# The down projection of an encoder layer in another order of its seven block products

## The reference, cut to what matters

```python
def encoder_forward(x, ...):
    h = rmsnorm(x, norm_mix); z = h @ w_in
    a = pool_mixer(z[..., :512], pool_maps, pool_scale) @ w_up_pool
    b = attention_branch(z[..., 512:]) @ w_up_attn
    gates = sigmoid(h @ w_gate + b_gate)
    x = x + (gates[..., :1024] * a + gates[..., 1024:] * b) @ w_out
    h = rmsnorm(x, norm_ffn)
    x = x + (silu(h @ w_ffn_gate) * (h @ w_ffn_up)) @ w_ffn_down     # 2816 inner channels
    return rmsnorm(x, norm_final)
y_prompt, y_sample = encoder_forward(x_prompt, ...), encoder_forward(x_sample, ...)
```

## Time and profile before

| | |
|---|---|
| median of 3 runs | 2657.43 us (2657.41 to 2657.67) |
| profiled execution | 2660.76 us, span 2659.0 us |
| PE busy | 2569.1 us, 97% of the span |
| POOL busy | 1846.2 us, 69% |
| DVE busy | 1231.4 us, 46% |
| ACT busy | 1066.4 us, 40% |
| down projection, first sequence | 1113.68 to 1349.74 us |
| first matmul of the second sequence's first product | 1366.77 us |
| down projection, second sequence | 2433.66 to 2647.8 us |

### The profile page before, as it was taken

One profiled execution on the slowest core, in us unless ns is written; L12 is line 12 of the kernel. 1 busy time (PEld: TensorE's weight loads), 2 busy tenths in 40 slices (PEclk: granted clock), 3 DMA queues, 4 the chain that ended last, 5 costly groups with the idle time before them and its releaser, 6 DMA issues. The chain is left out here.

```text
span 2659.0 us, 33336 instructions
## 1 busy us (share of the span) xinstructions
PE 2569.1 (97%) x12048; PEld 2107.3 (79%) x12048; DVE 1231.4 (46%) x1689; ACT 1066.4 (40%) x2084; POOL 1846.2 (69%) x1350
## 2 busy tenths in 40 slices
PE   6999999999899999999889999999998999999998
PEld 5888888788688888878778888887877888888786
DVE  6753455754322222354777434557443222223545
ACT  5224454443433333344542344545443332333444
POOL 6775445435688888798967653454457888887985
PEclk9999999999999999999999999999999999999999
DMA  3444444562233333464343434455612333334533
GB/s 128 126 133 120 140 142 138 170 244 79 80 95 119 96 106 97 136 205 159 115 163 106 151 106 141 150 160 157 246 67 80 107 96 118 97 105 156 183 123 139
DMA packets 334963, 350.76 MB, mean 132 GB/s; under 512 B 16849, under 2 KB 247633, under 8 KB 333265
## 3 DMA queue, kind: packets, MB, share of 16 engines
q1 hardware_dynamic: 331344, 338.03, 40.5%
q10 hardware_dynamic: 3456, 10.60, 1.0%
HBM read 249.28 MB, written 99.29 MB: 131 GB/s over the span
## 5 line engine op out<-in xcount | busy, mean ns | idle before, releaser
L903 PE MATMUL ps<-S,t_hi 128*128 128x512 f32 x2296 | 908.5, 396 | 7.7 <-DVE gst L1638 3.7
L905 PE MATMUL ps<-S,t_lo 128*128 128x512 f32 x2296 | 895.7, 390 | 0.0
L904 PE MATMUL ps<-S,t_hi 128*128 128x512 f32 x2296 | 894.8, 390 | 0.0
L903 PEld LDWEIGHTS ps<-S,t_hi 128*128 128x128 f32 x2296 | 432.0, 188 | 97.3 <-issue 6.6
L905 PEld LDWEIGHTS ps<-S,t_lo 128*128 128x128 f32 x2296 | 431.5, 188 | 92.4
L904 PEld LDWEIGHTS ps<-S,t_hi 128*128 128x128 f32 x2296 | 432.3, 188 | 86.1
L743 POOL TENSOR_TENSOR t_lo<-wraw,t_hi 128x512 fp32r<-128x512 f32 x190 | 246.8, 1299 | 241.2 <-ACT t_hi L1221 238.1
L743 POOL TENSOR_TENSOR t_lo<-wraw_ff,t_hi 128x512 fp32r<-128x512 f32 x220 | 282.7, 1285 | 77.0 <-ACT t_hi L1221 72.7
L1221 ACT CAST t_hi<-wraw_ff 128x512 fp32r<-128x512 f32 x220 | 137.0, 624 | 374.9 <-PE ps L905 372.2
L743 POOL TENSOR_TENSOR t_lo<-R,t_hi 128x512 fp32r<-128x512 f32 x154 | 232.4, 1514 | 60.5 <-ACT t_hi L1221 60.4
L1839 DVE TENSOR_TENSOR d_lo<-d_raw,d_hi 128x512 fp32r<-128x512 f32 x154 | 179.3, 1168 | 199.3 <-ACT d_hi L1409 199.1
(11 more groups left out here) (160 smaller groups left out, 4131.0 us busy)
## 6 DMA issues: line engine op xcount, KB each, us to landing
d_raw<-d_rows SPq DMA_DIRECT2D x154, 256.0 KB, 3.2
d_rows<-act_f SPq DMA_DIRECT2D x110, 256.0 KB, 2.1
wraw<-w_in SPq DMA_DIRECT2D x44, 512.0 KB, 6.0
wraw_ff<-w_ffn_gate SPq DMA_DIRECT2D x44, 512.0 KB, 4.8
wraw_ff<-w_ffn_up SPq DMA_DIRECT2D x44, 512.0 KB, 4.7
R<-w_ffn_down SPq DMA_DIRECT2D x88, 256.0 KB, 3.1
sp_rows<-gst SPq DMA_DIRECT2D x80, 256.0 KB, 2.4
wo_raw<-w_out SPq DMA_DIRECT2D x36, 512.0 KB, 3.3
```

What stands on the lines that cost most here:

```text
L903: nc.tensor.matmul(o_ps, w[0], r[0], start=begins, stop=False, skip_group_check=True)
L904: nc.tensor.matmul(o_ps, w[0], r[1], start=False, stop=False, skip_group_check=True)
L905: return nc.tensor.matmul(o_ps, w[1], r[0], start=False, stop=ends, skip_group_check=True)
```

## The change

The seven products come in the order A12, A11, S1, S2, S4, S3, A22 instead of A11, S1, S2, S4, S3, A12, A22. The even tiles have all their sums after the fifth product (step 54) instead of after the sixth. The weight quarter (1, 0) is loaded twice, for product 0 and again, one product ahead of its use, for product 6; loads now stand with products 0, 1, 2, 3 and 5. The final norm of the even tiles moves from product 6 (k = 2 to 10) to product 5 (k = 6 to 10), the stores to (5, 9) to (6, 1). The table `EARLY` begins one step later. The first norm of the last tokens moves from behind the last product into it (k = 8 to 10).

```diff
-DOWN = (("A11", 0, True, ((0, 0),)), ("S1", 1, True, ((1, 1),)), ("S2", 0, False, ((0, 1),)),
-        ("S4", 1, False, ((0, 1),)), ("S3", 0, False, ((1, 0), (1, 1))), ("A12", 1, True, ((0, 0),)),
+DOWN = (("A12", 0, True, ((0, 0),)), ("A11", 1, True, ((0, 0),)), ("S1", 0, True, ((1, 1),)),
+        ("S2", 1, False, ((0, 1),)), ("S4", 0, False, ((0, 1),)), ("S3", 1, False, ((1, 0), (1, 1))),
         ("A22", 0, True, ((1, 0),)))
-DOWN_LOADS = {0: (0, 0, 0), 1: (0, 1, 1), 2: (1, 1, 2), 5: (1, 0, 2)}
+DOWN_LOADS = {0: (1, 0, 0), 1: (0, 0, 1), 2: (0, 1, 2), 3: (1, 1, 0), 6: (1, 0, 0)}
-EARLY = {1: (0, 1, 2), 2: (3, 4), 3: (5, 6), 4: (7, 8), 5: (9, 10), 6: (11, 12), 7: (13,), 9: (14, 15), 10: (16,)}
+EARLY = {2: (0, 1, 2), 3: (3, 4), 4: (5, 6), 5: (7, 8), 6: (9, 10), 7: (11, 12), 8: (13,), 9: (14, 15), 10: (16,)}
             def load_rows(s, m):
-                if o not in DOWN_LOADS:
+                if o == 5:
+                    o = 6
+                elif o not in range(4):
                     return
...
-                    if o_next in (1, 2, 4):
+                    if o_next in (2, 3):
                         rows_sum(s, o_next, k_next)
                     low_part(s, m, rows_of(o, k))
-                    if o == 5:
-                        rows_sum(s, 5, k)
+                    if o in (4, 5):
+                        rows_sum(s, o + 1, k)
...
-                    if o == 6 and k in (2, 3, 6, 7):
-                        final_stats(s, (2, 3, 6, 7).index(k))
-                    if o == 6 and k in (5, 6, 9, 10):
-                        store_out(s, (5, 6, 9, 10).index(k))
+                    if o == 5 and k in (6, 7, 8, 9):
+                        final_stats(s, k - 6)
+                    if (o, k) in ((5, 9), (5, 10), (6, 0), (6, 1)):
+                        store_out(s, ((5, 9), (5, 10), (6, 0), (6, 1)).index((o, k)))
+                    if o == 6 and k == 8 and s + 1 < SEQS:
+                        first_stats(s + 1, 3)
...
-                    if o == 6 and k in (3, 4, 7, 8):
-                        final_norm(s, (3, 4, 7, 8).index(k))
+                    if o == 5 and k >= 7:
+                        final_norm(s, k - 7)
+                    if o == 6 and k >= 9 and s + 1 < SEQS:
+                        first_norm(s + 1, k - 3)
```

More of the change, by code:

```diff
@@ L153 @@
 DMA_SEMS.update({f"o_stored{n}": 12 for n in range(4)})
-DMA_SEMS.update({f"r_in{r}": 11 for r in range(4)})
+DMA_SEMS.update({f"r_in{r}": n for r, n in enumerate((14, 14, 14, 13))})
 DMA_SEMS.update({f"d_in{r}": n for r, n in enumerate((20, 19, 19, 19))})
@@ L599, in load_part @@
                 r = (m - N_PROD) % 4
+                if o == 0 and k == KC - 1:
+                    sp.wait_ge(a12_stored[0], due("a12_stored0", s, 6))
                 if m >= N_PROD + 4:
@@ L692, in _ @@
                 sp.wait_ge(ff_stored[1], due("ff_stored1", s, 30))
+                for r in range(2):
+                    sp.wait_ge(a12_stored[r], due(f"a12_stored{r}", s, 5))
                 for m in range(N_PROD, N_OPS):
@@ L804, in rows_sum @@
                 r1, r2, r3 = (R[r][k][:, :] for r in range(3))
[L805 to L809, removed]
+                if o == 2:
                     loaded(2)
                     pool.wait_ge(t_ready, due("t_ready", s, N_PROD + KC + k + 1))
-                    a, b, c = r1, r3, r1
-                elif o == 4:
+                    a, b, c = r2, r3, r2
+                elif o == 3:
+                    loaded(3)
+                    pool.wait_ge(t_ready, due("t_ready", s, N_PROD + 2 * KC + k + 1))
+                    a, b, c = r2, r1, r2
+                elif o == 5:
                     pool.wait_ge(t_made, due("t_made", s, PAIR_SUMS + k + 1))
-                    a, b, c = r2, r3, r2
+                    a, b, c = r3, r1, r3
                 else:
-                    pool.wait_ge(t_ready, due("t_ready", s, N_PROD + 2 * KC + k + 1))
-                    a, b, c = r1, r3, r1
+                    loaded(6)
+                    pool.wait_ge(t_ready, due("t_ready", s, N_PROD + 3 * KC + k + 1))
+                    a, b, c = r1, r1, r2
                 nc.gpsimd.tensor_tensor(a, b, c, ALU.subtract).then_inc(t_made, 1)
@@ L1541, in _ @@
                         part_his(s + 1, 0, EARLY.get(k - 1, ()))
[L1542 to L1545 removed]
+                    if o == 5 and k in (6, 7, 8, 9):
[4 more added lines that the diff above has]
+                        first_stats(s + 1, 3)
                 if s + 1 < SEQS:
[L1547 to L1549 removed]
+                    part_his(s + 1, 0, range(EARLY_DONE - 1, 21))
                 else:
@@ L1947, in _ @@
                         add_quarter(s, o - 1, 0)
-                    if k == 1 and o == 5:
+                    if k == 1 and o == 6:
                         add_quarter(s, o - 1, 1)
@@ L1951, in _ @@
                         part_low(s, m + 4)
-                    if o == 6 and k == 2:
+                    if o == 5 and k == 7:
                         dve.wait_ge(gfin_in, due("gfin_in", s, 1))
@@ L1963, in _ @@
                 if s + 1 < SEQS:
-                    part_los(s + 1, 0, range(EARLY_DONE - 1, 18))
-                    for t in (6, 7):
-                        first_norm(s + 1, t)
-                    part_los(s + 1, 0, range(18, 28))
+                    part_los(s + 1, 0, range(EARLY_DONE - 1, 28))
                 else:
```

18 lines of the change are left out of this document (8 added, 10 removed).

## The result

| | before | after |
|---|---|---|
| median of 12 runs each, side by side | 2660.22 us (2657.11 to 2662.57) | 2665.14 us (2660.99 to 2667.76) |
| profiled execution | 2660.76 us, span 2659.0 | 2665.62 us, span 2663.7 |
| PE / POOL busy | 97% / 69% | 96% / 70% |

What follows compares the result with a forecast made beforehand. PE bounds the kernel, losing time to POOL's pace and the turn. Sequence 0 at -0.9 and sequence 1 at +2.4 gave +1.5 us: 2658.9 us against a median of 2657.43, own range 2654 to 2663, over all 2650 to 2667.

Steps and rivals of the forecast that it cites:

- What bounds the kernel: Down projections: PE, busy 97%, loses time to POOL's pace once its lead is spent and to the turn between sequences.
- Steps 11 to 43, sequence 1: First sums start at step 21 with POOL 5.2 us ahead, losing 0.27 a step: 0.5 us lost instead of 3.99, -3.5.
- Steps 11 to 43, sequence 0: Weight rows queue behind token loads: PE waits 4.2 us at step 33, then nine steps at 2.96; +1.2 us.
- Steps 44 to 65: Less POOL lead (2.3 us) and norms beside pairs (a sum and a t_lo): +7.3 us in sequence 0, +5.9 in sequence 1.
- the strict sums of 3.23 and 4.51 us: Steps 44 to 65: pair of POOL instructions plus d_lo, without and with a norm, under exclusive port lock; not used in forecast.
- Product 6, sequence 0: First wait for DVE's S longer, second shorter, half-speed spell gone, a transposes' place saved: -1.2 us, bounds -5 and +5.
- one transposes' place later in EARLY saves a wait of about 1.5: Product 6 of sequence 0: the term that turned its sum from +0.3 us to -1.2.
- DVE's debt: Slower rival, product 6 of sequence 0: late DVE delays every S if the first wait exceeds some 6 us; 2665.4 us, chance 0.25.
- The turn: End of product 6 to sequence 1's second product: a chain over POOL takes 12.8 us instead of 21.03, -8.2.
- The double load: Product 5: 11 x 256 KB loaded where DMA is busy 0.44 of the time, used four steps after issue; costs nothing.
- POOL finds its beat: Faster rival, steps 44 to 65: sums hide and final norms cost POOL little, +3 and +1.5; 2650.2 us, chance 0.22.
- The turn does not shrink: Rival at the turn: last tokens' norms or POOL's sums still behind the end, gain only 4; 2663 us, chance 0.08.

Runs made afterwards that it cites:

- The spread loads: Changed kernel with the next sequence's seven token loads issued one at a time behind steps 12, 14, ... 24 instead of together behind step 33: 2657.43 us, ratio 0.9991.
- the five-step shift: Changed kernel with sums of weights for products 2 and 3 and the loads they need five steps earlier: 2663.31 us, ratio 1.0013.
- the norms moved out: Changed kernel with the even tiles' four final norms at steps 66 to 69 instead of 62 to 65, stores at 68 to 71: 2662.27 us, ratio 1.0004.
- the token loads moved: Changed kernel with the next sequence's seven token loads behind step 15 instead of step 33: 2662.69 us, ratio 1.0005.
- SP's order exchanged: Changed kernel with SP issuing the activation load ahead of the weight load in product 5: single run, 2660.65 us.
- all together: Changed kernel with five-step shift, spread token loads, first norms at steps 72 and 73, even tiles' statistics, norms and stores one step earlier: 2650.35 us, ratio 0.9965.
- the kernel with later first norms: Changed kernel with first norms of tiles 4 and 5 at steps 72 and 73 instead of 69 and 70: single run, 2660.34 us.

## Why the prediction was right and where it failed

**What bounds the kernel** was right: every wait of PE in the two down projections of after has one of the named releasers, t_lo (14.4 us in all), S (5.4), or the one I did not name, d_lo (1.4).

**Steps 11 to 43, sequence 1:** -3.3 for -3.5. The lead of 5.2 us and its loss of 0.27 a step held to a step.

**Steps 11 to 43, sequence 0:** +2.1 for +1.2. The wait (4.35 for 4.2) and its place were right. Behind it the price was wrong in kind and near in size: not nine steps at 2.96, but one step at half speed (4.97 us, 2.25 over), after which POOL had its lead back until step 41; 2.25 + 0.43 where I had 2.1. I had said that the lower clock is covered by POOL's pace; it was the larger part of the price. The spread loads confirmed that the whole stretch hangs on the burst.

**Steps 44 to 65:** +6.3 for +7.3 and +4.0 for +5.9. The mechanism is right, shown by the five-step shift (-3.6 and -2.7) and by the norms moved out (-1.5 and -1.1). The mis-sized term is the number of pairs that meet a norm inside the stretch. I charged three final norms in each sequence, but in sequence 1 they come so late that only step 65 is 3.92 us long; the next two meet their norm in product 6, where POOL has no sums. In sequence 0 six steps are at 3.9 us where I had seven.

As to how POOL and DVE disturb one another: a pair takes 2.95 us and with a norm 3.92 in after, as before, and the final norms cost POOL the same as the first norms. The norm itself takes 2.13 us instead of 1.28. The Trainium skill (SBUF — State Buffer, SBUF: two separate sides) has the shared port pair as an exclusive lock, held for the whole instruction; no run of steps with sums in these traces goes at the strict sums of 3.23 and 4.51 us. The measurement decides: both sides lose, but less than a full exclusion would cost.

**Product 6, sequence 0:** +1.5 for -1.2. The step that failed is "one transposes' place later in EARLY saves a wait of about 1.5", and a clock that I had not charged. Steps 67 to 69 grew by 3.6 us (5.00, 5.68 and 8.79 for 3.95, 6.70 and 5.21), where my terms gave +2.3, +1.7 and -1.5, together +2.5; 1.6 of them are the half speed in step 68, behind the wait of 2.12 for POOL. Steps 70 and 71 gave 3.0 back for the 3.7 of the forecast (the second wait is 0.81, as predicted). And steps 73 to 75 grew by 0.9: of the three groups of transposes taken out of step 67, one stands in step 68 now and one each in steps 73 and 74. A transpose moved is not a transpose saved. Three kernels with the same code in this product (the token loads moved, spread, and SP's order exchanged) took 47.54 to 47.55 us with step 68 at full speed (4.12 us); the five-step shift, also with the same code there, took 50.14 with step 68 at 6.34. So 2.0 of the 2.7 us missed come and go from one trace to the next, and why is not shown. The other 0.7 fits what steps 73 to 75 grew by.

**Product 6, sequence 1:** +2.1 for 0. I gave this stretch no term at all. The rival "DVE's debt" named the mechanism but put it in sequence 0 alone, where transposes wait; it bites in sequence 1 through d_lo. Kernels with this code took 31.97 to 32.00 us four times and 34.88 twice; with the final norms earlier (all together, 30.10; SP's order, 30.05) or the X adds ahead of them (final norms in product 6, 30.05) the wait is gone in each.

**The turn:** -8.2 for -8.2, with each link of the chain as predicted. Undoing it alone cost 4.7 us there.

**The double load:** 0 was predicted. No wait of PE is put down to it, but it is not free. Its wait for POOL stands on SP's queue ahead of the activation load. I had named SP's queue for the token loads and not here.

**The rivals.** "POOL finds its beat" fell with steps 44 to 65. "DVE's debt" happened in part: in its place, product 6 of sequence 0, the first wait was 4.59 us, under the 6 that I gave as its point, and the second 0.81, and the turn lost nothing. What DVE's lateness costs through d_lo, 2.1 us, lies in sequence 1. That the median lies near this rival's time is no support for it. "The turn does not shrink" fell. Had I put 2.1 us on sequence 1 and 0 on the moved transposes, the sum would have been +5.1, near the +4.7 of the spans, but in part by luck: the 2.9 us that I had too much on steps 44 to 65 stand against the half speed in step 68 and the price at step 33.

## What to carry to other kernels

When one engine's work per step is a little over the bound engine's, write down its lead at each block: the step at which waits begin, and what a gap of free steps is worth, follow from it to within a step. Moving the work spends the lead elsewhere: of the 3.6 and 2.7 us that the five-step shift gave in steps 44 to 65, 0.8 and 0.6 came back in steps 11 to 43. Charge an edit for everything that stands behind it on each in-order queue, including loads behind a new wait and the operands of the next product behind norms that now end later, also in the pass where the edit seems to have no part. Long transfers that nobody needs soon belong one by one between the short ones: here 3.5 MB in one piece cost 6.5 us, and spread over 12 steps nothing, until the short loads around them were doubled and the same spread loads cost some 2 us.

## What the runs showed of the hardware

- The same wait does not always bring the same clock: behind a wait of 2.12 us the matmuls of after fell to half speed (0.63 us shown for 0.39) from the seventh on, and behind one of 2.11 us in the kernel with later first norms they stayed at full speed.
- Runs of one kernel differ by 4 to 10 us from lowest to highest, more than this change's effect. Part of it arises in stretches whose code did not change: step 0 of sequence 0 began at 1111.6 to 1118.0 us, and product 6 of sequence 1 took 32.0 or 34.9 us with the same code.
- A load of 256 KB behind seven of 512 KB landed about 11 us after its issue, where the median of such loads is 3.1 us. Among spread loads of 512 KB and with two weight loads a step, one landed 7.2 us after its issue.
